# Attention logits in three fp32r products instead of one fp32 product, with the modulation groups placed anew

## The reference, cut to what matters

```python
# first block, layer i; xl: 512 latent rows, xc: 256 context rows
ml = modulation(c, w_mod[i], b_mod[i])          # silu(c) @ w_mod + b: 6 x 1024 columns
mc = modulation(c_ctx[None, :], w_mod[i], b_mod[i])
hl = modulate(rmsnorm(xl, g_pre_mix[i]), ml[0], ml[1])
hc = modulate(rmsnorm(xc, g_pre_mix[i]), mc[0], mc[1])
...
k_c, v_c = mla_keys_values(zc_kv, ...)          # 256 keys
k_l, v_l = mla_keys_values(zl[..., KV], ...)    # 512 keys
# latent rows: 512 queries on 768 keys; context rows: 256 queries on 256 keys
# per head: softmax(q @ k.T / sqrt(96)) @ v
y_l = mix_stream(zl, concat(k_c, k_l), concat(v_c, v_l), ...)
```

## Time and profile before

| what | value |
|---|---|
| time, median of 3 runs | 2936.13 us (2931.41 to 2937.1) |
| the profiled execution's own time | 2935.57 us |
| its span in the trace | 2934.2 us |
| TensorE matmul busy | 2836.1 us, 97% |
| VectorE / ScalarE / GpSimd busy | 46% / 38% / 44% |
| matmuls of L625 (fp32r, three products) | 9936, 2210.7 us busy |
| matmuls of L769 (logits) | 320, 105.6 us busy |
| matmuls of L653 (modulation) | 1536, 52.7 us busy |

### The profile page before, as it was taken

The page is one execution under the profiler, slowest core; times in us unless marked ns, Lnnn a source line. Parts: engine busy times, 40 slices in busy tenths (PEclk is TensorE's granted clock), DMA queues, the critical chain, the costliest instruction groups (busy, mean ns, idle before and its releaser), DMA issues.

```text
span 2934.2 us, 40890 instructions
## 1 busy us (share of the span) xinstructions
PE 2836.1 (97%) x16278; PEld 2341.0 (80%) x16278; DVE 1356.9 (46%) x2527; ACT 1125.4 (38%) x1917; POOL 1277.9 (44%) x828
## 2 busy tenths in 40 slices
PE   7789999999999999989999899999999999999999
PEld 6577778888888786778888787888878878888887
DVE  5448643241211576632211457776542368667432
ACT  4353554553332444543332344332433344323332
POOL 4253247874444442344444353343534433435343
PEclk9899999999999999999999999999999999999999
DMA  7834114653233324033333222111223221212222
GB/s 260 307 106 152 39 49 151 181 160 101 94 94 129 113 82 144 1 108 94 96 93 102 71 97 69 58 58 58 87 72 94 77 89 49 68 58 72 85 73 87
DMA packets 81981, 291.67 MB, mean 99 GB/s; under 512 B 9216, under 2 KB 9600, under 8 KB 81408
## 3 DMA queue, kind: packets, MB, share of 16 engines
q1 hardware_dynamic: 81792, 289.06, 30.6%
HBM read 286.93 MB, written 2.10 MB: 99 GB/s over the span
## 4 chain that ended last, share of the span: by engine, by line
PE 84%; DVE 10%; ACT 2%; issue 2%; POOL 1%; DMA 1%; SPq 0%; POOLq 0%; ACTq 0%; DVEq 0%
PE ps L625 65%; PE ps L598 5%; DVE ps L2263 4%; PE ps L769 3%; PE ps L790 2%; PE ps L958 1%; PE ps L653 1%; PE ps L1021 1%; PE ps L1032 1%; PE ps L894 1%; PE ps L1199 1%; DVE t L2555 1%; DVE t L2593 1%; POOL t L2895 1%; PE ps L907 0%
## 5 line engine op out<-in xcount | busy, mean ns | idle before, releaser
L625 PE MATMUL ps<-t,t 128*128 128x512 f32 (+3 forms) x9936 | 2210.7, 380 | 20.9 <-DVE t L2027 7.4
L625 PEld LDWEIGHTS ps<-t,t 128*128 128x128 f32 x9936 | 1778.5, 189 | 366.5 <-issue 33.1
L2895 POOL TENSOR_TENSOR t<-t,t 128x1024 fp32r<-128x1024 f32 (+3 forms) x444 | 1041.0, 2348 | 1105.4 <-ACT t L1335 1064.9
L1335 ACT ACTIVATE t<-t 128x1024 fp32r<-128x1024 f32 (+3 forms) x444 | 457.9, 1035 | 855.1 <-PE ps L625 806.0
L598 PE MATMUL ps<-t,t 128*128 128x128 f32 (+2 forms) x1662 | 237.5, 279 | 33.9 <-DVE t L2078 12.2
L598 PEld LDWEIGHTS ps<-t,t 128*128 128x128 f32 (+2 forms) x1662 | 190.4, 141 | 80.9 <-ACT t L1448 16.1
L2366 DVE TENSOR_TENSOR ps<-ps,t 128x512 f32<-128x512 f32 (+1 forms) x96 | 57.2, 606 | 344.1 <-ACT t L1641 344.1
L2379 DVE TENSOR_TENSOR t<-ps,t 128x512 f32<-128x512 f32 x60 | 40.9, 692 | 217.6 <-PE ps L625 217.5
L2263 DVE SCALAR_TENSOR_TENSOR ps<-t,t,ps 128x512 f32<-128x512 f32 (+1 forms) x174 | 116.1, 667 | 6.4 <-ACT ps L1556 0.6
L2915 POOL TENSOR_TENSOR t<-t,t 128x4 f32<-128x4 f32 (+2 forms) x93 | 85.6, 921 | 75.3 <-DVE t L2036 39.3
L769 PE MATMUL ps<-t,t 96*128 96x384 f32 (+1 forms) x320 | 105.6, 453 | 4.8 <-DVE t L2126 2.4
(11 more groups left out here) (264 smaller groups left out, 2398.8 us busy)
## 6 DMA issues: line engine op xcount, KB each, us to landing
t<-in_wbig SPq DMA_DIRECT2D x412, 512.0 KB, 3.5
t<-in_wmod SPq DMA_DIRECT2D x96, 512.0 KB, 6.5
t<-in_wbig SPq DMA_DIRECT2D x16, 416.0 KB, 3.2
t<-in_wbig SPq DMA_DIRECT2D x14, 256.0 KB, 2.7
t<-in_wbig SPq DMA_DIRECT2D x8, 332.0 KB, 3.0
t<-in_wbig SPq DMA_DIRECT2D x6, 384.0 KB, 3.1
t<-in_x SPq DMA_DIRECT2D x1, 2048.0 KB, 8.2
out<-t SPq DMA_DIRECT2D x8, 256.0 KB, 2.1
```

Of the source, the lines that this page charges most:

```text
L625: m = p.matmul(out, lhs, rhs, start=kk == 0 and n == 0, stop=kk == tiles - 1 and n == 2)
L1335: a.activation(c.hi(w), c.raw(w), ACT.Copy).then_inc(w_hi.h, w_hi.up(("cut", w)))
L2895: g.tensor_tensor(c.lo(w), c.raw(w), c.hi(w).bitcast(F32), ALU.subtract).then_inc(w_lo.h, w_lo.up(("cut", w)))
```

## The change

1. The logits of the three attentions are computed as high query by high key, high query by low key and low query by high key, in fp32r. In l0 and l1 a unit has 6 matmuls of 384 columns, in c0 3 of 256 columns.
2. The copies of the head load are on ScalarE now (high parts of queries and keys); VectorE forms the low parts by subtraction from PSUM, and waits for ScalarE's copy each time. TensorE's logits wait for both low parts. A PSUM bank of a head load comes free with VectorE's subtraction, where it was ScalarE's copy for the queries. The low parts lie in AL, the high queries in AH, for c0 all in the old QT and KT.
3. ScalarE's order: the copy of the remaining keys (`load_rest`) stands behind the exponential of unit u (u % 4 is 2) and ahead of the copy of unit u-1's probabilities. On VectorE the subtraction stands where the copy stood.
4. Modulation groups: (0,5) to (0,8) among c0's heads (rate 0.25), (0,9) and (0,10) in and after `mix("l0")`, (0,11) and (1,0) to (1,4) after units 3, 8, 13, 18, 23 and 28 of l0, (1,7) to (1,9) after units 4, 9 and 14 of l1. The buffer sets change: nearly all groups from (0,9) on use set 0, so that a group's DMAs start when the group before is done. The DMAs of (0,4) and (0,5) are issued earlier (behind the tiles of `zt` and of `sc` of c0), that of (0,10) waits for the end of `sb` of l0.

```diff
@@ fetches
-                if u == (0, 4):
-                    return at[("w", self.of[("sc", "c0")][q])]
+                if u in ((0, 4), (0, 5)):
+                    return at[("w", self.of[("zt" if u[1] == 4 else "sc", "c0")][q])]
...
@@ mod_set
-        if n < 13:
-            return (0, 1, 2, 3, 0, 2, 4, 0, 2, 4, 0, 4, 0)[n]
-        return {17: 3, 23: 1}.get(n, 4 if n % 2 else 0)
+        if n < 9:
+            return (0, 1, 2, 3, 0, 2, 4, 0, 2)[n]
+        return {10: 4, 17: 3, 23: 1}.get(n, 0)
...
+    def head_parts(self, n, h):
+        Q, K, b = self.QT[h % 2], self.KT[h % 2], h % 2
+        if n == "c0":
+            return Q[:, 0:256], Q[:, 256:512], K[:, 0:256], K[:, 256:512]
+        low = self.AL[0:96, 0:3, :].rearrange("p k n -> p (k n)")
+        return Q, self.AH[0:96, b, :], K, low[:, 768 * b:768 * b + 768]
...
@@ TensorE, logits
-            for j in range(2):
-                k0, kn = j * nh, min(nh, nk * 128 - j * nh)
-                m = p.matmul(Q[:, 512 * j:512 * j + kn], c.QT[b][:, 128 * t:128 * t + 128], c.KT[b][:, k0:k0 + kn],
-                             start=True, stop=True)
+            for m, (qp, kp) in enumerate(((QH, KH), (QH, KL), (QL, KH))):
+                for j in range(na):
+                    last = p.matmul(Q[:, 512 * j:512 * j + nh], qp[:, 128 * t:128 * t + 128],
+                                    kp[:, nh * j:nh * j + nh], start=m == 0, stop=m == 2)
...
@@ ScalarE, attention
+            A.wait_ge(turned, ("kt", n, h, 0))
+            a.activation(KH[0:64, 0:w], Q[0:64, 512:512 + w], ACT.Copy).then_inc(act.h, act.up(("kh", n, h, 0)))
+
+        def load_rest(h):
+            for k0 in k0s[1:]:
+                w = 128 * (nk - k0)
+                A.wait_ge(turned, ("kt", n, h, k0))
+                a.activation(KH[0:64, 128 * k0:128 * k0 + w], Q[0:64, 0:w], ACT.Copy).then_inc(
+                    act.h, act.up(("kh", n, h, k0)))
...
             if u < n_u:
                 logits(u)
+            if u % nt == 2 and u // nt + 1 < NH:
+                load_rest(u // nt + 1)
             if 1 <= u <= n_u:
                 turn(u - 1)
...
@@ VectorE, load_head and load_rest
-            V.wait_ge(turned, ("kt", n, h, 0))
-            v.tensor_copy(c.KT[h % 2][0:64, 0:w], c.pair(("head", n, h))[0:64, 512:512 + w]).then_inc(
+            V.wait_ge(act, ("qt", n, h))
+            v.tensor_tensor(QL[:, 0:T], Q[0:96, 0:T], QH[:, 0:T].bitcast(F32), ALU.subtract).then_inc(
+                dve.h, dve.up(("ql", n, h)))
+            V.wait_ge(act, ("kh", n, h, 0))
+            v.tensor_tensor(KL[0:64, 0:w], Q[0:64, 512:512 + w], KH[0:64, 0:w].bitcast(F32), ALU.subtract).then_inc(
                 dve.h, dve.up(("ktr", n, h, 0), ("kt", n, h)))
...
-                V.wait_ge(turned, ("kt", n, h, k0))
-                v.tensor_copy(c.KT[b][0:64, 128 * k0:128 * k0 + w], Q[0:64, 0:w]).then_inc(
-                    dve.h, dve.up(("ktr", n, h, k0), ("kt", n, h)))
+                V.wait_ge(act, ("kh", n, h, k0))
+                v.tensor_tensor(KL[0:64, at:at + w], Q[0:64, 0:w], KH[0:64, at:at + w].bitcast(F32),
+                                ALU.subtract).then_inc(dve.h, dve.up(("ktr", n, h, k0), ("kt", n, h)))
...
@@ the order of the stages, the same on all engines
-    rest = onward(weave(heads("c0"), mods(0, 5, 12, [6, 7]), 0.45, -1.0), 2 * NH + 2)
+    rest = onward(weave(heads("c0"), mods(0, 5, 9, [6, 7]), 0.25, -1.0), 2 * NH + 2)
-    run(beside(weave(mix("l0"), g, 0.5), mods(1, 0, 1, [2, 6]), (56,)))
-    run(mods(1, 1, 2, [2, 3]))
-    rest = onward(beside(heads("l0"), mods(1, 2, 5, [6, 7]), (4, 5, 12)), 4 * NH + 2)
+    run(beside(weave(mix("l0"), g, 0.5), mods(0, 9, 10, [2, 6]), (56,)))
+    run(mods(0, 10, 11, [2, 3]))
+    groups = chain(mods(0, 11, 12, [6, 7]), mods(1, 0, 5, [6, 7]))
+    rest = onward(beside(heads("l0"), groups, (3, 8, 13, 18, 23, 28)), 4 * NH + 2)
-    rest = onward(beside(heads("l1"), mods(1, 7, 10, [6, 7]), (4, 5, 12)), 4 * NH + 2)
+    rest = onward(beside(heads("l1"), mods(1, 7, 10, [6, 7]), (4, 9, 14)), 4 * NH + 2)
```

More of the change, by code:

```diff
@@ L1433, in attention @@
     def attention(n, nk, nt, tail):
+        k0s = list(range(0, nk, 4))
         def load_head(h):
+            QH, QL, KH, KL = c.head_parts(n, h)
+            Q, w = c.pair(("head", n, h)), 128 * min(4, nk)
             A.wait_ge(turned, ("qt", n, h))
@@ L1937, in act_program @@
     run(steps)
-    rest = onward(weave(heads("c0"), mods(0, 5, 12), 0.45, -1.0), 2 * NH + 2)
+    rest = onward(weave(heads("c0"), mods(0, 5, 9), 0.25, -1.0), 2 * NH + 2)
     row_of("c0")
@@ L1942, in act_program @@
     run(beside(weave(project("c0"), both(rest, g, 4), 1.0), only(g, 3), (11, 14, 15)))
-    run(beside(weave(mix("l0"), g, 0.5), mods(1, 0, 1), (56,)))
-    run(mods(1, 1, 2))
-    rest = onward(beside(heads("l0"), mods(1, 2, 5), (4, 5, 12)), 4 * NH + 2)
+    run(beside(weave(mix("l0"), g, 0.5), mods(0, 9, 10), (56,)))
+    run(mods(0, 10, 11))
+    groups = chain(mods(0, 11, 12), mods(1, 0, 5))
+    rest = onward(beside(heads("l0"), groups, (3, 8, 13, 18, 23, 28)), 4 * NH + 2)
     row_of("l0")
@@ L2864, in dve_program @@
     run(mods(1, 6, 7))
-    rest = onward(beside(heads("l1"), mods(1, 7, 10), (4, 5, 12)), 4 * NH + 2)
+    rest = onward(beside(heads("l1"), mods(1, 7, 10), (4, 9, 14)), 4 * NH + 2)
     next(rest)
@@ L3236, in pool_program @@
     run(beside(weave(project("c0"), both(rest, steps, 4), 1.0), only(steps, 3), (11, 14, 15)))
-    run(beside(weave(mix("l0"), then(steps, residual, "c0"), 0.6), mods(1, 0, 1), (56,)))
-    run(mods(1, 1, 2))
-    rest = onward(beside(heads("l0"), mods(1, 2, 5), (4, 5, 12)), 4 * NH + 2)
+    run(beside(weave(mix("l0"), then(steps, residual, "c0"), 0.6), mods(0, 9, 10), (56,)))
+    run(mods(0, 10, 11))
+    groups = chain(mods(0, 11, 12), mods(1, 0, 5))
+    rest = onward(beside(heads("l0"), groups, (3, 8, 13, 18, 23, 28)), 4 * NH + 2)
     next(rest)
```

71 lines of the change are left out of this document (43 added, 28 removed).

## The result

The changed kernel takes 2971.79 us (median of 4, 2970.73 to 2977.86) against 2936.52 us (4 runs of before): a ratio of 1.013, 95% interval 1.0118 to 1.0142. It is slower by some 35 us; I had said 2940, in a range up to 2957. The profiled execution took 2972.11 us, with a span of 2970.8 against 2934.2.

The account below looks back on a forecast made before the run. Bound: TensorE's work and waits, paced by a three-engine chain in light units; chain and DMAs in c0. Relay with shorter logits +15, groups -2.4, c0 -8: +4.6 us on 2935.57, so 2940 us, range 2919 to 2957.

Parts of the forecast that it names:

- The light half of the relay: Units 18 to 21, walked through the engines' queues from logits(18): logits(22) at 11.1 us, 9.73 before, so +1.4 us.
- The saving on TensorE: Logits in l0 and l1: fp32r saves 0.29 us a unit, 18.6 us over 64 units, where TensorE is the bound.
- my line: Line through fp32r prices at 512 and 256 columns: 384 columns take 0.175 to 0.18 us, a unit's six 1.05.
- The heavy half: Units 22 to 25, which also multiply values: logits(26) at 28.3 us against 26.38 in the walk, so +0.5 us.
- The first heads: Start of each layer: +0.5 us for the first head's uncovered relay, +0.5 for the second head's rotated keys copied twice.
- +7.4: Relay and shorter logits over one layer, l0 or l1: +7.4 us, +15 for both.
- Together -2.4: Modulation groups in l0 and l1, partly in TensorE's idle holes: 6.2 against 5.9 us and 3.1 against 5.9.
- costed the DMAs at nothing: Modulation weights' DMAs, now following each other in one set: no cost; some us of waiting if the cover fails.
- a forecast of -8: c0: earlier weights -4.7, three groups fewer -6, shorter logits -2, relays +4.2 and +0.5; bounds -13 and -2.
- C: Slower: ScalarE's queue at head changes doubles the hole before valued(21), 1.2 us at each of 14: 2957 us, chance 0.22.
- A: TensorE is the bound in l0 and l1 and queues don't matter: -29 us, 2909 us with uncovered relays, chance 0.12.
- D: c0's clock stays at 1.2 GHz longer with less TensorE work: +12 us against the sum, 2952 us, chance 0.08.

Follow-up runs that it names:

- e2: Changed kernel with the old head load and no low parts (all three products read the high ones, so its result is not the program's): 2929.37 us.
- e3: Kernel before, with only the changed kernel's modulation group places, buffer sets and DMA order: 2939.43 us, ratio 1.0012.
- e1: Changed kernel with its modulation groups moved to other units of l0 and l1, where both head banks were to be free: 2965.07 us, ratio 1.0099.
- e9: e10 with the modulation weights of (0,4) and (0,5) asked for one stage later: 2935.96 us, ratio 0.9999.
- e6: Changed kernel with the group places of e1 and the early remaining-keys copy of e5 together: 2950.99 us, ratio 1.0059.
- e7: e6 with the second head's two rotated-key copies moved behind unit 0's maximum, and two l0 groups one unit earlier: 2952.37 us, ratio 1.0058.
- e10: e3 with its groups after the 4th, 9th, 12th, 17th, 20th and 28th unit of l0 and 12th, 20th and 28th of l1: 2936.03 us.
- e12: e9 with the weights of (0,5) asked for as late as in the kernel before: 2934.51 us, ratio 0.9995.
- e4: Changed kernel with only the first of the three logits products, every copy, subtraction and wait kept: 2973.47 us, ratio 1.0128.
- e5: Changed kernel with ScalarE's copy of the remaining keys moved ahead of the same unit's exponential: 2958.94 us, ratio 1.0079.

## Why the prediction was wrong, point by point

I forecast +4.6 us and the profiled executions differ by 36.6. The step that failed most is the price of the groups (point 5), then that of the relay over a layer (points 3 and 4). The steps, by their own terms:

1. **The light half of the relay: right.** The walk put maximum(18) at 2.3 and found 2.27, the exponential at 3.5 (3.42), transposes at 4.5 (4.46), maximum(19) at 5.5 (5.63), logits(22) at 11.1 (11.07). Only logits(20) came 0.66 later than walked, behind VectorE's copy of probabilities, and cost nothing, since the next chain was longer still.
2. **The saving on TensorE: mis-sized, though not by the line.** From a unit's first logits matmul to its first values matmul it is now 1.23 and 1.24 us (357.99 to 359.22 in l0, 1223.88 to 1225.12 in l1), where it was 1.39: 0.15 us a unit, not 0.29. The starts within the unit say where the rest went (the first, second and last logits matmul and the first values):

```profile
1223.88 0.42 PE L778 MATMUL ps<-t,t 96*128 96x384 f32 x1
1224.14 0.34 PE L778 MATMUL ps<-t,t 96*128 96x384 f32 x1
...
1224.85 0.34 PE L778 MATMUL ps<-t,t 96*128 96x384 f32 x1
1225.12 0.33 PE L799 MATMUL ps<-t,t 128*64 128x128 f32 x2
```

   and before:

```profile
365.07 0.49 PE L769 MATMUL ps<-t,t 96*128 96x384 f32 x1
365.40 0.48 PE L769 MATMUL ps<-t,t 96*128 96x384 f32 x1
...
366.04 0.49 PE L769 MATMUL ps<-t,t 96*128 96x384 f32 x1
366.46 0.33 PE L790 MATMUL ps<-t,t 128*64 128x128 f32 x2
```

   From the second to the last the fp32r matmuls start 0.71/4 = 0.178 us apart, as my line had it (0.175 to 0.18; the 0.229 in it should have been 0.225, 11.15 less a tail over 48, which hardly moves it). What I had left out are the ends: the first distance is 0.26, some 0.08 more than the pace, and the switch to the values is 0.09 in both kernels, not 0.05. The heavy half shows the smaller saving: 17.73 where the walk gave 17.2. e2 against e3 says the same: 16.01 for 16.64 over four such units. The Trainium skill (TensorE: Matmul & The Clock Gate, Back-to-back issue gap) has N/2.4 + 2.5 ns for an isolated matmul, an estimate of 0.163 us at 384 columns and 0.98 a unit; the trace's 0.178 is further from it than from my line.
3. **The first heads: mis-sized most.** I gave the first head +0.5 and the second head's rotated copies +0.5. Units 0 to 8 of l1 hold no group in e1 and in e9: 29.0 us and 23.0. That is +6.0 where my terms make 2.9 (one light half 1.4, one heavy 0.5, the two extras). Unit 3 to 4 makes 3.2 of it (5.47 for 2.26). ScalarE's order is 1.8 of that, since in e6 it is 3.66; the rest would fit VectorE's copies of the rotated keys, 1.74 us from start to end where one of 0.55 had stood, but e7, which moved them, brought nothing. Units 4 to 6 make another 1.8 (7.07 for 5.31), and that is the clock, which fell behind the longer unit 3 to 4: it is 0.57 there in e1, and in e6, at 1.00, they take 5.20.

```profile
1166.03:1173.10 7.07, 7.07 (x32) 6.74 (x33) 4.37 (x12) 4.56 (x12) 2.05 (x4) 0.57 0.01 2
```

4. **A layer then costs +12, not +7.4.** In l1 the three groups take 0.94, 2.12 and 3.89 us (units 0 to 8, 29.94 for 29.00 in e1, both with some us at a low clock; unit 8 to 9, 6.37 for 4.25; units 13 to 16, 15.67 for 11.78, from the same places of a later head). Without these 6.95 the stretch is 109.8 us, and before, without three groups of 1.93, it was 97.6. Twice +12.2 is 24.4, for the +15 of the sum.
5. **The groups: the step that failed.** "Together -2.4" counted their work, and let it fall into holes. By the line above six in l0 cost 126.04 - 109.79 = 16.25 and three in l1 6.95, so 23.2 for 11.6 before: +11.6, which is 14.0 off. I had looked for a hole in TensorE's time and not for who holds the bank: a group waits for VectorE's last step on it, and holds the logits behind it. The new head load is not what makes this dear in sum, though single waits got longer (1.61 for 0.78 behind unit 17). In e3, with the old head load and the same places, the same reckoning gives 114.7 - 97.6 = 17.1 for the six and 7.6 for the three, 24.7 together. The places and the number of groups cost this with either head load, and e10 shows that better places take 4.7 of it away. By differences of kernels the split is much the same: places +13.1 (e3 less before) for -2.4, relay and products together +22.9 (after less e3) for +15. I had costed the DMAs at nothing, which was right: no wait for modulation weights in l0 or l1.
6. **c0: right in the heads, wrong ahead of them.** -7.6 for a forecast of -8, though its parts were others (the places alone gave -14.0, the relay took 9.0, both with a part of the clock in them), so that this sum came right is partly luck. But the first logits came 5.4 us later, for which I had +0.5. Most of it is not the relay's: kernels without any relay start at 95.9 to 97.5, e12 with before's order of DMAs among them. Its cause stays open.
7. Between the stretches and behind them +2.8, not forecast and not explored.

The misses add up: 9.4 for the relay, 14.0 for groups, 0.4 in c0's heads, 5.4 ahead (0.5 of it is in the sum of -8), 2.8: 32.0, which is 36.6 less 4.6.

Of the rivals, C had the right sign and the right queue. Its place was wrong: the hole before valued(21) did not double from 1.2 us, it is 0.70 in l1, and VectorE's copy ends it. The queue hurts in the light half, at VectorE's wait for the rest (as I had walked), and at the banks. A is ruled out by e4 and by the stretches; D's clock was 0.85 in c0, as before (0.84), but it did fall where TensorE had been kept waiting in l0. What I named as a sign for C, stretches beyond 118 us, came true in l0 (126.0), not in l1 (116.7).

## What to carry to other kernels

A piece of work put into a hole of an engine in strict order costs the wait for its own buffers, with everything behind it: ask who reads the PSUM bank out before it, not only how busy the engine is. Nine such groups cost 23.2 us for the 9.3 that I had added up. When a copy becomes copy-and-subtract over two engines, place each half by who waits for it; one line of ScalarE's order was worth 13 of 35 us here. And measure a change in its parts: places, arithmetic and relay were +3.4, -10.1 and +42.4 us, and a detail of the first, the earlier DMA, was alone the only complete version to come out ahead of both, by 2.8 us. And look at the clock of a stretch before two profiles are compared: 2.2 of the 2.5 us between e6 and e7 in l1 were that.

## What the runs showed of the hardware that I had not expected

- **The clock falls behind a wait, and on little work.** The group that had waited 4.63 us in l0 ran in 3.58 us instead of 1.93. The windows of that group and of the 4 us ahead of it:

```profile
303.49:307.07 3.58, 3.58 (x65) 2.23 (x65) 0.46 (x2) 0.00 (x0) 0.00 (x0) 0.52 0.00 0
299.00:303.00 4.00, 0.00 (x0) 0.00 (x0) 2.61 (x5) 1.74 (x4) 3.64 (x5) 0.64 0.00 0
```

 A granted clock of 0.52 is the lower level, 1.2 GHz; before's l0 had 1.00 throughout. So a stall of this size was paid for twice: the wait, and 1.65 us on the next piece of work. In e4, with the least work on TensorE, l1 had a mean of 0.86. Not each such wait is followed by a fall: after 2.83 us of waiting a group ran at half speed in l1 of e5, and after 2.82 us one ran at full speed in its l0.
- **384 columns in fp32r** take 0.178 us a matmul at their pace (point 2), on the line between 256 and 512 columns (0.13 and 0.23), but the first distance of each six is 0.26. Before, in fp32, it is 0.33 for a pace of 0.32. Why it is longer wasn't tried.
- **A copy to fp32r within SBUF was slow on VectorE only while GpSimd worked beside it:** 32x768 took 0.75 and 1.07 us in after (CAST, above), with GpSimd busy from 301.30 to 303.03 but for 0.09 us, and 0.55 and 0.54 in e7, where GpSimd did nothing at that time. The fp32 copy of the same shape (COPY, L2131 of before) took 0.55 with GpSimd busy all through.

```profile
1142.96 0.55 DVE L2176 CAST t<-t 32x768 fp32r<-32x768 f32 x1
```
